# A convolution in rows from shifted copies, in the state-space stage of a hybrid decoder layer

## The chip, the cores and the metric

The kernel runs on one core of a Trainium2 chip. The metric is the device time of one execution in microseconds; of three runs the median counts.

## What is computed

One decoder layer for 256 tokens of width 2048, in float32. x is normalised, projected by one wide matrix, and goes through two mixers, a Mamba-2 branch and a differential attention; both are merged and projected, and a SwiGLU network follows. The change lies in the Mamba-2 branch:

```
xbc = silu(causal_depthwise_conv(xbc, conv_w, conv_b))      # 4 taps along the sequence
xs, Bm, Cm = split(xbc, ...)                                 # xs: 8 groups x 8 heads x 64
dt = softplus(dt_raw + dt_bias);  A = -exp(a_log)
y = ssd_chunked(xs, dt, A, Bm, Cm) + d_skip * xs             # one chunk of 256 tokens
# in it: cb = C @ B^T;  y_diag = (cb * decay) @ (xs * dt),  decay = exp(a_cs[l] - a_cs[s]) for l >= s
y = y * silu(z);  y = y * rsqrt(mean(y * y over the group) + eps) * norm_w
```

The convolution makes out[t, c] = b[c] + sum over j of w[j, c] * x[t - 3 + j, c], with nothing before t = 0.

## The kernel before

Every large product is made in **units**: two blocks of 128 rows of the weights by 512 columns. SP loads a unit's weights (512 KB) into one of four ring slots, w_raw (`load`, line 410). ScalarE rounds them to w_hi (`split_hi`, L724), VectorE makes the remainder w_lo (`split_lo`, L1257), and TensorE multiplies twelve times (`rows_unit`, L2246): high by high, high by low, low by high, for two blocks of the rows and two tiles of 128 tokens. A slot of w_hi is written once the unit four back has been multiplied (mm_done), a slot of w_raw once its remainder is made (lo_ready). So ScalarE and VectorE run up to four units ahead of TensorE. Each engine carries out its instructions in order, and semaphores are all that ties them together: the code of every engine says after which unit u of which chunk each small step stands.

The stage that is changed loops over eight groups g. A group is 16 units: eight make the x columns of the group (chunk x, into acc 0) and eight the z columns (chunk z, into acc 1). I call them x0 to x7 and z0 to z7. Because of the lead of four, the step that ScalarE or VectorE has "at u" of a chunk stands behind the split of the unit four later: u = 0 of chunk z behind the split of z4, u = 4 of chunk z behind that of the next group's x0. On TensorE "at u" is behind unit u itself. On SP the last load of chunk z stands at u = 7.

What happens to a group beside its units:

- ScalarE evicts chunk x, scaled by each token's factor, to x_proj, in rows (tokens on partitions). TensorE turns it into columns (channels on partitions) by eight transposes into acc 0, after z0. ScalarE writes the last tap and the bias from there to conv_x (`conv_first_taps`), VectorE adds the other three taps (`conv_taps`, L1447, twelve operations, one input in PSUM), the shift along the sequence being a shift along the free dimension. ScalarE applies silu, and after z4 TensorE turns conv_x back into rows by eight transposes. VectorE multiplies them by dt (xdt, L1682), ScalarE copies them to y_row, and GpSimd multiplies that by d_skip (L2199).
- GpSimd loads a_cs by broadcast from DRAM (acs_b, L2185) and adds a mask (L2193), ScalarE makes the decays by an exponential (`exps`, L977, at u = 2 and 3 of chunk z), VectorE multiplies them by cb (`decays`, L1658, at u = 3 and 4).
- In chunk x of the next group TensorE makes the decay products (`y_products`, L2549) after x1, ScalarE copies them out, and after x3 TensorE makes `y_rows` (transposes, and the product L2562). VectorE adds and gates (`tail_gated`), ScalarE sums the squares, GpSimd makes the factor, VectorE applies it (`tail_normed`, L1624), TensorE turns it into columns after z0, VectorE stores them to yT.

A VectorE operation that reads what the one before it wrote waits for that by a semaphore (`link`).

Of the kernel before, what the change touches and what calls it, by code (L numbers as in the profile page):

```python
# [28 lines left out]
ALU = mybir.AluOpType  # L29
# [3 lines left out]
P = 128  # L33
T = 256
# [150 lines left out]
def layer(nc, x, mix_norm_w, w_in, conv_w, conv_b, dt_bias, a_log, d_skip, ssm_norm_w, w_ssm_proj,  # L185
# [3 lines left out]
    with ctx:  # L189
# [6 lines left out]
        def sem(name):  # L196
# [77 lines left out]
        conv_x = at("conv_x", 191, [P, CT, T])  # L274
# [66 lines left out]
        conv_first, conv_done = sem("conv_first"), sem("conv_done")  # L341
        sq_read = sem("sq_read")
        bc_rows_ready, bc_T, x_rows_ready, x_T = sem("bc_rows_ready"), sem("bc_T"), sem("x_rows_ready"), sem("x_T")
# [14 lines left out]
        xs_ready, xs_T, xdt_ready, xrow_ready, skip_ready = (sem(n) for n in (  # L358
            "xs_ready", "xs_T", "xdt_ready", "xrow_ready", "skip_ready"))
# [39 lines left out]
        def _(sp):  # L399
# [302 lines left out]
        def _(act):  # L702
# [232 lines left out]

            def tail_columns(g):
# [4 lines left out]
            def x_chunk(g, head):  # L941
                for u in range(UPC):
                    split_hi()
                    if u == 1 and not head:
                        tail_columns(g - 1)
# [8 lines left out]
                    if u == 4 and not head:  # L954
                        tail_squares(g - 1)
# [10 lines left out]
                last.then_inc(x_rows_ready, 1)  # L966

            def exps(g, hf, head):

                act.wait_ge(acs_masked, g * 2 + (hf + 1))  # L970
                if hf == 0 and not head:
# [9 lines left out]
            def z_chunk(g, head):  # L981
                for u in range(UPC):
                    split_hi()
                    if u == 0:

                        act.wait_ge(x_T, g + 1)
                        for n in range(CT):
                            last = conv_first_taps(sums(0)[:, n], g * CT, conv_x[:, n], n)
                        last.then_inc(conv_first, 1)
# [3 lines left out]
                    if u == 2:  # L993
                        act.wait_ge(conv_done, g + 1)
                        nc.scalar.activation(conv_x[:], conv_x[:], ACT.Silu).then_inc(xs_ready, 1)
                        exps(g, 0, head)
                    if u == 3:
                        exps(g, 1, head)
                    if u == 5:

                        act.wait_ge(xdt_ready, g + 1)
                        nc.scalar.activation(y_row[:], side[:, 2:4], ACT.Copy).then_inc(xrow_ready, 1)
# [14 lines left out]
            for c in range(4):  # L1017
                for u in range(UPC):
                    split_hi()
                    if c == 0 and u == 1:  # L1020
# [1793 lines left out]
```

## Time and profile before

| what | value |
|---|---|
| median of three runs | 2049.43 us (2049.01 to 2050.93) |
| profiled execution | 2051.72 us, span of the trace 2050.1 us |
| busy share TensorE, VectorE, ScalarE, GpSimd | 100%, 76%, 57%, 8% |
| granted TensorE clock | 1.00 |
| DMA | 419.80 MB, 205 GB/s on average |
| the changed stage | about 592 to 1024 us of the span |

The span is the time from the first to the last instruction of the profiled execution. TensorE is busy nearly all the time, so the other engines' busy shares say little by themselves: what counts is whether each step is there when TensorE comes to it.

### The profile page before, as it was taken

Reading aid. Unit: us, or ns where it says so; the run is one execution under the profiler, and the core shown is the slowest. Engines: PE = TensorE matmul, PEld = TensorE weight load, DVE = VectorE, ACT = ScalarE, POOL = GpSimd, SP = SyncE. Lnnn points to the kernel's source line nnn. Section 1 sums busy time; section 2 is a strip of 40 time slices with the busy share of each in tenths; the row PEclk is TensorE's granted clock in tenths of the full one; section 3 lists DMA queues with packets and bytes.
Section 4 is the critical chain, followed back from the end, with each engine's and each line's share of the span. In section 5 each row is a group of like instructions: output and inputs, shape, how many; then the busy total and the mean of one; then the engine's idle time right before and its main releaser. Section 6 shows DMA issues by size and latency. Waiting matters only on the chain.

```text
span 2050.1 us, 28075 instructions
## 1 busy us (share of the span) xinstructions
PE 2040.8 (100%) x9580; PEld 1677.7 (82%) x9580; DVE 1566.3 (76%) x1861; ACT 1172.0 (57%) x1496; POOL 171.6 (8%) x195
## 2 busy tenths in 40 slices
PE   9999999999999999999999999999999999999999
PEld 8888877778888888888888888888888888887887
DVE  6777866665856777777667887888898889877866
ACT  5444655555556666666655554556666666645543
POOL 1121000000011222222000000010000000000000
PEclk9999999999999999999999999999999999999999
DMA  7656675654566666666565657598888888667574
GB/s 250 199 182 203 188 220 166 176 162 152 182 204 186 185 185 184 185 190 187 167 192 183 212 168 238 177 307 244 258 254 237 250 259 250 196 205 232 176 246 154
DMA packets 220626, 419.80 MB, mean 205 GB/s; under 512 B 16449, under 2 KB 22002, under 8 KB 220290
## 3 DMA queue, kind: packets, MB, share of 16 engines
q1 hardware_dynamic: 212162, 399.48, 61.8%
q0 software_dynamic: 7776, 18.94, 4.4%
q8 instruction: 47, 0.77, 0.2%
q10 hardware_dynamic: 608, 0.34, 0.1%
q14 instruction: 33, 0.27, 0.0%
HBM read 410.25 MB, written 4.26 MB: 202 GB/s over the span
## 4 chain that ended last, share of the span: by engine, by line
PE 92%; DVE 3%; DMA 2%; ACT 1%; issue 0%; SPq 0%; DVEq 0%; ACTq 0%
PE acc L2246 72%; PE side L2333 8%; PE acc L2333 6%; PE side L2262 3%; DMA w_raw<-in_w_ffn_down 1%; DVE w_lo L2038 1%; PE side L2402 1%; PE side L2549 1%; DVE w_raw L1953 0%; ACT w_hi L1216 0%; DVE w_lo L1257 0%; DMA x_row<-in_x 0%; DMA w_raw<-in_w_in 0%; PE acc L2262 0%; ACT w_hi L724 0%
## 5 line engine op out<-in xcount | busy, mean ns | idle before, releaser
L1257 DVE TENSOR_TENSOR w_lo<-w_raw,w_hi 128x1024 fp32r<-128x1024 f32 x332 | 420.7, 1280 | 245.7 <-ACT w_hi L724 244.5
L724 ACT ACTIVATE w_hi<-w_raw 128x1024 fp32r<-128x1024 f32 x332 | 348.5, 1057 | 355.7 <-PE acc L2246 315.2
L2246 PE MATMUL acc<-w_hi,h_hi 128*128 128x512 f32 x1248 | 498.7, 400 | 0.2
L2246 PE MATMUL acc<-w_hi,h_lo 128*128 128x512 f32 x1248 | 487.0, 390 | 0.0
L2246 PE MATMUL acc<-w_lo,h_hi 128*128 128x512 f32 x1248 | 485.9, 389 | 0.0
L2246 PEld LDWEIGHTS acc<-w_hi,h_hi 128*128 128x128 f32 x1248 | 234.4, 188 | 52.7 <-issue 7.0
L2246 PEld LDWEIGHTS acc<-w_hi,h_lo 128*128 128x128 f32 x1248 | 234.3, 188 | 50.3
L2246 PEld LDWEIGHTS acc<-w_lo,h_hi 128*128 128x128 f32 x1248 | 234.7, 188 | 47.6 <-issue 1.9
L1932 DVE TENSOR_TENSOR w_lo<-w_raw,w_hi 128x1024 fp32r<-128x1024 f32 x136 | 165.1, 1220 | 38.0 <-ACT w_hi L1137 35.4
L1053 ACT ACTIVATE w_hi<-w_raw 128x1024 fp32r<-128x1024 f32 x110 | 116.6, 1061 | 117.2 <-PE acc L2246 70.2
L1137 ACT ACTIVATE w_hi<-w_raw 128x1024 fp32r<-128x1024 f32 x136 | 142.9, 1057 | 65.8 <-PE acc L2246 50.4
L1216 ACT ACTIVATE w_hi<-w_raw 128x1024 fp32r<-128x1024 f32 x102 | 107.8, 1060 | 106.5 <-DMA w_raw<-in_w_ffn_down 57.4
L1734 DVE TENSOR_TENSOR w_lo<-w_raw,w_hi 128x1024 fp32r<-128x1024 f32 x110 | 132.2, 1223 | 47.3 <-ACT w_hi L1053 45.4
L1137 ACT ACTIVATE w_hi<-side_raw 128x1024 fp32r<-128x1024 f32 x100 | 106.2, 1062 | 98.1 <-PE acc L2246 45.2
L2038 DVE TENSOR_TENSOR w_lo<-w_raw,w_hi 128x1024 fp32r<-128x1024 f32 x102 | 122.6, 1223 | 47.9 <-ACT w_hi L1216 46.8
L2246 PE MATMUL acc<-w_hi,x2T_hi 128*128 128x512 f32 x384 | 150.9, 393 | 0.5 <-DVE w_lo L1932 0.5
L2246 PE MATMUL acc<-w_hi,x2T_lo 128*128 128x512 f32 x384 | 149.6, 389 | 0.0
L2246 PE MATMUL acc<-w_lo,x2T_hi 128*128 128x512 f32 x384 | 149.4, 389 | 0.0
L1932 DVE TENSOR_TENSOR w_lo<-side_raw,w_hi 128x1024 fp32r<-128x1024 f32 x100 | 122.1, 1221 | 18.3 <-ACT w_hi L1137 16.6
L2246 PE MATMUL acc<-w_hi,a_hi 128*128 128x512 f32 x252 | 98.2, 390 | 0.0
L2246 PE MATMUL acc<-w_hi,a_lo 128*128 128x512 f32 x252 | 98.1, 389 | 0.0
L2246 PE MATMUL acc<-w_lo,a_hi 128*128 128x512 f32 x252 | 98.1, 389 | 0.0
(436 smaller groups left out, 3445.9 us busy)
## 6 DMA issues: line engine op xcount, KB each, us to landing
w_raw<-in_w_in SPq DMA_DIRECT2D x320, 512.0 KB, 4.3
w_raw<-in_w_ffn_down SPq DMA_DIRECT2D x88, 512.0 KB, 4.9
w_raw<-in_w_ffn_gate SPq DMA_DIRECT2D x68, 512.0 KB, 4.6
w_raw<-in_w_ffn_up SPq DMA_DIRECT2D x68, 512.0 KB, 5.2
w_raw<-in_w_ssm_proj SPq DMA_DIRECT2D x64, 512.0 KB, 4.4
side_raw<-in_w_ffn_up SPq DMA_DIRECT2D x40, 512.0 KB, 4.7
w_raw<-in_w_attn_proj SPq DMA_DIRECT2D x32, 512.0 KB, 3.7
w_raw<-in_w_out SPq DMA_DIRECT2D x32, 512.0 KB, 4.7
```

The source lines that it names most:

```text
L724: nc.scalar.activation(w_hi[:, r], w_raw[:, n % RING], ACT.Copy).then_inc(hi_ready, 1)
L1053: nc.scalar.activation(w_hi[:, unit.slot % RING], w_raw[:, source], ACT.Copy).then_inc(hi_ready, 1)
L1137: nc.scalar.activation(w_hi[:, unit.slot % RING], ffn_source(names, name), ACT.Copy).then_inc(hi_ready, 1)
L1216: nc.scalar.activation(w_hi[:, unit.slot % RING], w_raw[:, source], ACT.Copy).then_inc(hi_ready, 1)
L1257: nc.vector.tensor_tensor(w_lo[:, r], w_raw[:, n % RING], w_hi[:, r].bitcast(F32), ALU.subtract).then_inc(lo_ready, 1)
L1734: nc.vector.tensor_tensor(w_lo[:, r], w_raw[:, source], w_hi[:, r].bitcast(F32), ALU.subtract).then_inc(lo_ready, 1)
L1932: nc.vector.tensor_tensor(w_lo[:, r], ffn_source(names, names[n]), w_hi[:, r].bitcast(F32), ALU.subtract).then_inc(lo_ready, 1)
L2038: nc.vector.tensor_tensor(w_lo[:, r], w_raw[:, source], w_hi[:, r].bitcast(F32), ALU.subtract).then_inc(lo_ready, 1)
L2246: done = nc.tensor.matmul(acc[p][:, t], a[:, k0 + kk, cut], w[:, r, kk], start=first and kk == n == 0, stop=last and kk == UK - 1 and n == ...
L2262: return nc.tensor.transpose(out_at, in_, ident)
L2333: done = nc.tensor.matmul(out_at, a, w[:, r, kk], start=first and kk == n == 0, stop=last and kk == UK - 1 and n == 2, skip_group_check=se ...
L2402: last = nc.tensor.matmul(side[:, 1 + m, first:first + width], qkT[half, 0, q * P:(q + 1) * P], qkT[half, 1, 0:width], start=True, stop=True)
```

## The change

The convolution is made in rows. With tokens on partitions, the row one, two or three tokens earlier lies on another partition, so SP copies x_proj from SBUF to SBUF, shifted by one, two and three partitions, into three tiles `earlier`. Partitions 16 to 127 of each go in three copies of 448 KB, then comes the weight load of z7, then six small copies: rows up to partition 15, and the first rows of the second tile of tokens from the last partitions of the first. VectorE sets the rows before t = 0 to zero once. GpSimd loads the group's taps and bias by broadcast over the partitions (`taps_load`, 4 x 2 KB and 2 KB a partition). VectorE multiplies each of the four tiles by its taps and adds them and the bias: eight operations over 128 x 1024 with both inputs in SBUF, behind the splits at u = 2 to 5 of chunk z. ScalarE applies silu in place at u = 6. So the sixteen transposes per group, conv_x, the taps' evictions and the copy to y_row are gone; xdt and the skip product read x_proj.

Moved: the exponentials from u = 2 and 3 to 4 and 5 (they also wait for taps_read, since taps_b lies in decay's place), the decay products with cb on VectorE from 3 and 4 to 6 and 7, xdt from u = 5 of chunk z to u = 0 of the next chunk x, y_products from x1 to x4, y_rows from x3 to x6, the gated tail from 3 to 6, the squares from u = 4 of chunk x to u = 0 of chunk z, y's scaling from VectorE (u = 6 of chunk x) to ScalarE (u = 2 of chunk z), y's transposes from z0 to z3, their store from u = 1 to 4. acc 0 is freed by ScalarE after the eviction. On GpSimd the order becomes: loads, skip, masks, wait for y_sum, taps, tail.

```diff
 SP, group i
-                chunk(w_in, (i + i) * (CW // 2) + COL_Z)
+                for u in range(UPC):
+                    if u == UPC - 1:
+                        sp.wait_ge(x_rows_ready, i + 1)
+                        for back in range(1, TAPS):
+                            sp.dma_start(earlier[back - 1][16:P], x_proj[16 - back:P - back]).then_inc(shift_in, 16)
+                    load(w_in, u * UK, (i + i) * (CW // 2) + COL_Z)
+                for back in range(1, TAPS):
+                    sp.dma_start(earlier[back - 1][back:16], x_proj[0:16 - back]).then_inc(shift_in, 16)
+                    sp.dma_start(earlier[back - 1][0:back, 1], x_proj[P - back:P, 0]).then_inc(shift_in, 16)
...
 ScalarE
+            def conv_silu(g):
+                act.wait_ge(conv_ready, g + 1)
+                nc.scalar.activation(x_proj[:], x_proj[:], ACT.Silu).then_inc(xs_ready, 1)
+            def tail_normed(g):
+                act.wait_ge(y_rstd, g + 1)
+                for t in range(TT):
+                    last = nc.scalar.activation(y_row[:, t], y_row[:, t], ACT.Copy, scale=y_scale[:, t:t + 1])
+                last.then_inc(y_ready, 1)
...
+                if not head:
+                    act.wait_ge(xdt_ready, g)
+                    act.wait_ge(skip_ready, g)
                 for t in range(TT):
                     last = nc.scalar.activation(x_proj[:, t], acc[0][:, t], ACT.Copy, scale=x_rstd[:, t:t + 1])
...
             def exps(g, hf, head):
                 act.wait_ge(acs_masked, g * 2 + (hf + 1))
+                if hf == 0:
+                    act.wait_ge(taps_read, g + 1)
...
+                    if u == 0 and not head:
+                        tail_squares(g - 1)
+                    if u == 2 and not head:
+                        tail_normed(g - 1)
+                    if u in (4, 5):
+                        exps(g, u - 4, head)
+                    if u == 6:
+                        conv_silu(g)
...
 VectorE
+            def by_taps(tile, back):
+                return nc.vector.tensor_tensor(tile[:], tile[:], taps_b[:, TAPS - 1 - back].unsqueeze(1).broadcast_to([P, TT, CW]), ALU.mult)
+            def conv_step(g, u):
+                if u == 2:
+                    dve.wait_ge(shift_in, g * 144 + 144)
+                    dve.wait_ge(taps_in, g * 32 + 32)
+                    by_taps(earlier[0], 1)
+                    by_taps(earlier[1], 2)
+                if u == 3:
+                    by_taps(earlier[2], 3)
+                    by_taps(x_proj, 0).then_inc(taps_read, 1)
+                if u == 4:
+                    dve.wait_ge(taps_read, g + 1)
+                    nc.vector.tensor_tensor(earlier[0][:], earlier[0][:], earlier[1][:], ALU.add)
+                    link(nc.vector.tensor_tensor(x_proj[:], x_proj[:], earlier[2][:], ALU.add))
+                if u == 5:
+                    link(nc.vector.tensor_tensor(x_proj[:], x_proj[:], earlier[0][:], ALU.add))
+                    nc.vector.tensor_tensor(x_proj[:], x_proj[:], conv_bias_b[:].broadcast_to([P, TT, CW]), ALU.add).then_inc(conv_ready, 1)
+            def tail_step(g, u):
+                if u == 0:
+                    x_scaled(g)
+                if u == 6:
+                    tail_gated(g)
...
+                    if u == 4 and not head:
                         tail_transposed(g - 1)
+                    conv_step(g, u)
+                    if u in (6, 7):
+                        decays(g, u - 6)
...
 GpSimd
+            def taps_load(g):
+                ours = conv_w[0][:, bass.ds(g * CW, CW)]
+                pool.dma_start(taps_b[:], ours.partition_broadcast(P)).then_inc(taps_in, 16)
+                pool.dma_start(conv_bias_b[:], conv_b[:, bass.ds(g * CW, CW)].partition_broadcast(P)).then_inc(taps_in, 16)
...
+            def next_group(i, first=False):
                 pool.wait_ge(decay_exp, i * 2 + 2)
                 loads(i + 1)
+                skip(i, first)
+                masks(i + 1)
+                pool.wait_ge(y_sum, i + 1)
+                taps_load(i + 1)
                 tail(i)
...
 TensorE
-                    if u == 1:
+                    if u == 4:
                         y_products(g)
-                    if u == 3:
+                    if u == 6:
                         y_rows(g)
...
-                        if not first:
-                            y_columns(g - 1)
-                    if u == 4:
-                        pe.wait_ge(xs_ready, g + 1)
-                        if not first:
-                            pe.wait_ge(yT_ready, g)
-                        for n in range(CT):
-                            for t in range(TT):
-                                last = transpose(side[:, 2 + t, n * P:(n + 1) * P], conv_x[:, n, t * P:(t + 1) * P])
-                        last.then_inc(xs_T, 1)
+                    if u == 3 and not first:
+                        y_columns(g - 1)
+                    if u == 6 and not first:
+                        pe.wait_ge(yT_ready, g)
```

## Rows read from the trace of the kernel before

**Rows 1.** Windows: us, busy us by engine, PEclk, DMA share, GB/s.

```profile
697.50:702.00 4.50, 4.50 (x21) 3.70 (x21) 2.87 (x3) 2.86 (x3) 0.00 (x0) 1.00 0.95 289
702.00:705.00 3.00, 3.00 (x17) 2.27 (x16) 1.20 (x2) 1.06 (x1) 0.00 (x0) 1.00 1.03 387
755.54:806.30 50.76, 50.76 (x264) 42.04 (x263) 37.58 (x40) 32.63 (x51) 11.70 (x9) 1.00 0.61 188
```

**Rows 2.** Chain of waits, one group: start us, length us, what.

```profile
704.79 13.65 PE acc L2246 x60
718.44 0.87 PE acc L2262 x8
...
720.84 10.91 PE acc L2246 x48
731.75 0.87 PE side L2262 x8
...
746.24 1.90 PE side L2549 x32
...
753.81 0.88 PE side L2262 x8
754.68 0.86 PE side L2562 x2
```

**Rows 3.** ScalarE's timeline, same group: start us, us, operation.

```profile
715.75 1.06 ACT L724 ACTIVATE w_hi<-w_raw 128x1024 fp32r<-128x1024 f32 x1 [1.35 <-PE acc L2246]
716.72 1.25 ACT L965 ACTIVATE x_proj<-acc,small 128x512 f32<-128x512 f32 x2
...
727.31 1.04 ACT L995 ACTIVATE conv_x<-conv_x 128x1024 f32<-128x1024 f32 x1
728.37 1.28 ACT L977 ACT_TABLE_LOAD   x1
729.67 2.45 ACT L977 ACTIVATE decay<-acs_b,neg_acs 128x128 f32<-128x128 f32 x8
```

**Rows 4.** VectorE's timeline, same group.

```profile
706.23 1.22 DVE L1614 TENSOR_TENSOR y_row<-side,y_row 128x1024 f32<-128x1024 f32 x1
707.48 0.69 DVE L1616 TENSOR_TENSOR y_row<-xdt_end,y_row 128x512 f32<-128x512 f32 x1
...
711.79 1.22 DVE L1257 TENSOR_TENSOR w_lo<-w_raw,w_hi 128x1024 fp32r<-128x1024 f32 x1 [1.22 <-ACT w_hi L724]
714.13 2.23 DVE L1257 TENSOR_TENSOR w_lo<-w_raw,w_hi 128x1024 fp32r<-128x1024 f32 x1 [1.11 <-ACT w_hi L724]
716.28 3.02 DVE L1624 TENSOR_SCALAR y_row<-y_row,small 128x512 f32<-128x512 f32 x2
...
721.66 5.24 DVE L1447 SCALAR_TENSOR_TENSOR conv_x<-acc,taps,conv_x 128x255 f32<-128x255 f32 x12
...
738.67 1.22 DVE L1257 TENSOR_TENSOR w_lo<-w_raw,w_hi 128x1024 fp32r<-128x1024 f32 x1
739.81 1.28 DVE L1682 TENSOR_TENSOR xdt<-side,dt 128x512 f32<-128x512 f32 x2
...
743.13 3.31 DVE L1257 TENSOR_TENSOR w_lo<-w_raw,w_hi 128x1024 fp32r<-128x1024 f32 x2 [1.22 <-ACT w_hi L724]
```

**Rows 5.** GpSimd's timeline, same group.

```profile
712.13 6.49 POOL L2193 TENSOR_TENSOR acs_b<-acs_b,cst 128x1024 f32<-128x1024 f32 x2
742.33 3.03 POOL L2199 TENSOR_TENSOR y_row<-y_row,d_skip_b 128x512 f32<-128x512 f32 x2 [23.71 <-ACT y_row L1002]
745.30 1.16 POOL L2185 DMA_DIRECT2D acs_b<-acs_scratch  x2
```

**Rows 6.** DMA issues: queue, count, size, median us to landing.

```profile
w_raw<-in_w_in SPq DMA_DIRECT2D x320, 512.0 KB, 4.3
...
acs_b<-acs_scratch POOLq DMA_DIRECT2D x16, 512.0 KB, 6.8
```

**Rows 7.** Line 410: ns min, median, max of an issue.

```profile
L410 SPq DMA_DIRECT2D w_raw<-in_w_in x320: 367/373/2333, 1.4 to 1067.5; - x160
```

More of the change, by code:

```diff
@@ L273, in layer @@
         x_proj = at("x_proj", 187, [P, TT, CW])
-        conv_x = at("conv_x", 191, [P, CT, T])
+        earlier = [at(f"earlier{n + 1}", kb, [P, TT, CW]) for n, kb in enumerate((138, 142, 175))]
+        taps_b = at("taps_b", 167, [P, TAPS, CW])
+        conv_bias_b = at("conv_bias_b", 191, [P, 1, CW])
         y_row = at("y_row", 195, [P, TT, CW])
@@ L1602, in _ @@
                 nc.vector.tensor_tensor(gated, acc[c % 2][:], gated, ALU.mult).then_inc(acc_free[c % 2], 1)
+            for back in range(1, TAPS):
+                last = nc.vector.memset(earlier[back - 1][0:back, 0], 0.0)
+            link(last)
             def tail_gated(g):
@@ new lines, in x_scaled @@
+            def x_scaled(g):
+                by_head = "p (h d) -> p h d"
+                dve.wait_ge(xs_ready, g + 1)
+                for t in range(TT):
+                    last = nc.vector.tensor_tensor(
+                        xdt[:, t].rearrange(by_head, d=HP), x_proj[:, t].rearrange(by_head, d=HP),
+                        dt[:, t, bass.ds(g * HG, HG)].unsqueeze(2).broadcast_to([P, HG, HP]), ALU.mult)
+                last.then_inc(xdt_ready, 1)
+                dve.wait_ge(xdt_ready, g + 1)
+                nc.vector.tensor_tensor(
+                    xdt_end[:].rearrange(by_head, d=HP), xdt[:, 0].rearrange(by_head, d=HP),
+                    edge[:, 0, bass.ds(g * HG, HG)].unsqueeze(2).broadcast_to([P, HG, HP]), ALU.mult).then_inc(xdt_end_ready, 1)
@@ L1694, in _, with z_chunk @@
+            def z_chunk(g, head):
+                for u in range(UPC):
+                    split_lo()
+                    if u == 4 and not head:
+                        tail_transposed(g - 1)
+                    conv_step(g, u)
+                    if u in (6, 7):
+                        decays(g, u - 6)
             x_chunk(0, True)
+            dve.wait_ge(edge_ready, 1)
             z_chunk(0, True)
@@ L2205, in _ @@
             pool.dma_start(acs_dram[:], acsT[:]).then_inc(acs_out, 16)
+            taps_load(0)
             pool.wait_ge(acs_out, 16)
             loads(0)
[L2208 to L2209 removed]
+            masks(0)
+            def next_group(i, first=False):
                 pool.wait_ge(decay_exp, i * 2 + 2)
                 loads(i + 1)
+                skip(i, first)
+                masks(i + 1)
+                pool.wait_ge(y_sum, i + 1)
+                taps_load(i + 1)
                 tail(i)
[L2214 removed]
+            next_group(0, True)
+            with repeat(pool, G - 2, [(own, 2)]) as i:
+                next_group(i + 1)
+            skip(G - 1)
             tail(G - 1)
```

118 lines of the change are left out of this document (26 added, 92 removed).

## The prediction

> **What bounds the kernel now.** First the windows view of one group of the stage that the change touches: TensorE is busy 50.76 of 50.76 us at full granted clock, VectorE 37.6, ScalarE 32.6, GpSimd 11.7, the DMA engines 61% [rows 1]. Then the chain of waits over one group: only TensorE, with nothing between its pieces [rows 2]. A group's period is therefore TensorE's work: 16 units, 13.65 us for five, so 2.72 each and 43.5 in all, and 7.2 us of small products and transposes between them. Last, the timelines of ScalarE, VectorE and GpSimd [rows 3 to 5], to see how far ahead of TensorE they run. That decides this change: it takes work from TensorE and gives VectorE more.
>
> The lead: ScalarE starts a unit's high part 0.2 us after the matmuls of the unit four back are done, and takes 1.06; VectorE's low part takes another 1.14 (the step from one operation to the next; the listed 1.22 overlap) [rows 3, 4]. TensorE needs it 3 units = 8.16 us after that same boundary, so VectorE may be 5.7 us late before TensorE stops.
>
> **TensorE's part.** Out go eight transposes of x_proj and eight of conv_x per group, 0.87 us each lot [rows 2]. The number of breaks in the matmul stream stays four (after units z0, z3, x4, x6), so what a break costs remains. Gain 1.74 us a group, 8 groups: 13.9 us. Period 50.76 - 1.74 = 49.0 if nobody stops TensorE.
>
> **The clock of one group.** I set T=0 where unit x7 ends and z0 begins, and put the new order on it. TensorE: z0 done 2.7; the scores and the break cost 0.66 + 0.1 (718.44 to 720.84 in the old group, less two lots of 0.87 [rows 2]); z1 done 6.2, z2 8.9, z3 11.6; y's transposes 1.0; z4 15.3, z5 18.1, z6 20.8, z7 23.5, x0 26.2, x1 28.9, x2 31.7, x3 34.4, x4 37.1. There the decay products stand, 1.97 with their break; after x6, y's rows, 1.8.
>
> **Copies.** ScalarE evicts x_proj at 1.2 to 2.4 as before (1.25 us [rows 3]). SP waits for that in front of the last z load, which it could otherwise issue at 2.8 (low part of z3), so the load is only 1 us later and isn't needed before 11.8: free. The copies carry 3 x 112 x 4 KB and small ones, 1.56 MB, a resource of which before has no like; the load adds 0.52. At 387 GB/s (a burst of weight loads) that is 5.4 us; GpSimd's new taps load (1.31 MB of broadcast) goes out at y's sum, -2.7. Its like is acs_b: 1.05 MB that land 6.8 us after issue [rows 6], in the burst that moves 289 GB/s [rows 1]; 3.6 us of that is data, so 3.2 are lead, and the taps' data start at 0.5, just ahead of the copies, and take 4.5. 0.5 + 4.5 + 5.4 + 0.5 of completion (my estimate) = 10.9; all of it at 289 gives 12.7; no clash gives 9.5. VectorE asks for the copies after its low part of z6, at 11.35. I take 0.3 us of waiting, nearer to the first value since most of the bytes are no broadcast, bounds 0 and 1.4; a copy from SBUF to SBUF at half the rate would make it 3.5. SP issues a load in 0.37 us [rows 7], so nine copies hold it some 4 us; the next load, x0, wanted landed by 15.5, goes out at 6.5 and lands at 10.8 by the median of 4.3 [rows 6], some 3 us later behind the queue: free.
>
> **VectorE.** Its tail of group g-1 comes at x6: y's sum is there at -2.7, low z2 ends at -2.1, four operations take 3.7, so low z3 ends at 2.8 and it then idles in wait of TensorE. Out: twelve tap steps (5.24) and y's scaling (3.02, of which 0.95 is work) [rows 4]; the latter goes to ScalarE at z2, ready at 11.3, and TensorE asks at 11.6: free by a hair. In: four products and four sums of 128x1024, 1.14 each, 1.25 where a wait for its own result follows (706.23 to 707.48) [rows 4]. In order from 11.35: product, product, low z7, product, product (17.05: taps_read), low x0, y's columns, sum, sum (21.7), low x1 (its high part comes at 21.9, since the exponentials now wait for taps_read, then take 1.28 + 2.36 [rows 3]), sum, sum (25.5), low x2, decay product (27.7). ScalarE's silu needs a table load and 1.04, ready 27.9, high part of x3 at 28.85.
>
> **Who shares with GpSimd.** GpSimd is given skip (two halves) once x is ready at 27.9, and masks when acs_b has landed: loads issued 24.3, 6.8 us [rows 6], 31.1. In the trace such an operation and one of VectorE with two SBUF inputs exclude each other and take turns [rows 4, 5]: a low part ends at 713.01, the next one, started at 714.13, ends at 716.36 having worked its own 1.1, so the first mask ran from 713.0 to 715.3; the second has 716.36 to 718.62, and the scaling started at 716.28 gets nowhere until then. So 2.27 us of VectorE's time for a mask. For a skip half 1.0: the pair lasts 3.03 with one low part in between, and two low parts beside it take 3.31 instead of 2.36. The old tap steps read PSUM and one SBUF tile; twelve went by in 5.24 us, none stretched. All the new ones read two SBUF tiles, and x's scaling by dt now does too. So after 27.7: skip half (to 29.0), low x3 30.15, skip half, decay product 32.3, mask, low x4 35.7, mask, x's scaling 1.28: done at 39.3. If the masks come later they still fall before it.
>
> The Trainium skill has this as a rule ("SBUF — State Buffer", Who interferes with whom): a VectorE instruction with two SBUF inputs contends with a GpSimd one that reads SBUF, whoever issues second blocks fully, and one with a single SBUF input doesn't contend. The rows agree, and it speaks against this change, which turns one-input work into two-input work. Without that rule the chain would end 5.5 us earlier, and the first rival would be the forecast.
>
> **Sum.** TensorE reaches the decay products at 37.1 and gets xdt at 39.3: 2.2 us lost a group, part of it already at x4 (35.7 against 34.4). Against that stands 1.74. The stall falls on groups 1 to 6: 13.2. Group 0 has no y columns on VectorE: 1.1. Group 7 has no masks behind it: none. Waiting for copies 7 x 0.3 = 2.1. Together -13.9 + 14.3 + 2.1 = +2.5 us. The profiled execution's span of 2050.1 becomes 2052.6 and its time of 2051.72 becomes 2054.2; that time stands 2.3 above the median of 2049.43, so the median becomes 2051.9, say 2052. Free, by what hides them: masks are done at 38 and used 28 us later; GpSimd has issued taps by -1.3 and the sums of squares that its tail waits for come at 5.2; TensorE's new wait for yT at z6 (19.4 against 20.8); the eviction's new wait for xdt and skip (both done ten us before it); ScalarE's wait for conv_ready, behind which high x3 is queued (28.9, low part 30.15, wanted 31.7; if GpSimd takes one turn more there, 1 us appears at x3 and is the same us that is lost later). ScalarE's lost evictions (y_row, first taps) pay for nothing, as it isn't late where they stood; its table loads stay two a group.
>
> **Rivals.**
> 1. VectorE comes in time and all of the gain shows. For: it was idle 13 of 50.8 us, and needs only 37.6 - 5.2 - 3.0 + 9.3 = 38.7 of 49. Against: its idle time lies at 3 to 10, before the copies are there; behind them it must run 17 operations plus GpSimd's turns in 25.7 us. It would take GpSimd's masks to land behind x's scaling (9 us instead of 6.8 from issue) or an alternation kinder than the one read. 2049.4 - 13.9 = 2035.5; half of it, 2043.
> 2. Slower: the copies land late. Every us beyond 11.35 moves the whole VectorE chain and costs 7 us in all; from 0.6 us it is slower by over 0.2%. Place: the wait after low z6. With copies at half the rate, landed at 13.5 to 14.8: 2052 + 13 to 22, 2065 to 2074 at the end. For: broadcast and copies meet on the same DMA engines, and the small ones come last. Against: a burst reaches 387 GB/s. The Trainium skill ("DMA: Bandwidth & Descriptors", Anatomy of one DMA) gives each DMA some 2 us of fixed cost; nine in a row would be 18 us and a far larger stall. Loads that land in 4.3 us while one goes out every 2.7 overlap theirs, so I leave that out.
> 3. A weight load or y's scaling is late by the new traffic (margins 3 us and 0.3 us): TensorE then stops at z3 too, but part is given back at x4. 2054 to 2060.
> That the change doesn't do what it says is no rival: the transposes are gone from the instruction stream.
>
> **How the numbers follow.** Measurement tells 0.2%, 4 us. Forecast (chain ends 2.2 late) 45%, own range 2046 to 2057; rival 1 25%; rival 2 22%; rival 3 8%. The range takes rival 1 down to 2037 and rival 2 up to 2065. Faster by over 0.2% (under 2045.3): rival 1 and a sliver, 28%. Slower (over 2053.5): rivals 2 and 3 and the upper end of the forecast, 36%. Within: 36%.
>
> **What would show it.** Right: the sixteen transposes gone; TensorE idle about 2 us a group, ahead of the decay products, released by VectorE's xdt or w_lo; period 51 us; VectorE without a gap from the shift wait to x's scaling; its operations beside masks stretched by 2 us. Rival 1: period 49.0, no wait. Rival 2: VectorE's first tap product waits for DMA for over 0.6 us. Wrong at the root: new two-input products that take another time than 1.14, or masks that land elsewhere.

## The result: 3.4% slower, and the profile after

The changed kernel takes 2119.65 us (median; 2114.64 to 2122.49), the kernel before 2050.11 on the same chip: ratio 1.0337, 95% interval 1.0316 to 1.0358. That is 69.5 us slower, and outside the range. The profiled execution has a span of 2120.9 us and a mean granted clock of 0.986.

The windows view of one group of the changed stage, where [rows 1] had 50.76 us. The first row is the whole group, the others are pieces of it. Columns as there: us, busy us of TensorE, its weight loads, VectorE, ScalarE, GpSimd, granted clock, DMA share, GB/s.

```profile
787.04:847.48 60.44, 53.00 (x247) 42.31 (x247) 42.67 (x35) 31.50 (x49) 13.31 (x11) 0.94 0.74 204
...
803.40:806.00 2.60, 2.53 (x13) 2.25 (x14) 0.05 (x1) 0.02 (x1) 0.00 (x0) 0.78 1.05 228
806.00:810.00 4.00, 4.00 (x14) 3.16 (x14) 0.00 (x0) 0.08 (x1) 0.00 (x0) 0.71 1.05 224
...
814.30:818.90 4.60, 0.12 (x2) 0.07 (x1) 4.60 (x5) 2.29 (x5) 0.00 (x0) 0.96 0.44 119
818.90:824.00 5.10, 5.10 (x16) 4.10 (x17) 4.72 (x5) 5.10 (x15) 0.00 (x0) 0.70 0.39 104
```

A group takes 60.44 us instead of the forecast 51.2. TensorE is idle for 7.44 of them, and busy for 53.00 instead of 49.0, most of it because its granted clock is down behind its two stops. The DMA engines are busy all the time from 803.4 to 810 and move only 224 to 228 GB/s; the burst of [rows 1] moved 387 at nearly the same share.

The waits of the whole run, by who waited for what: us in total, times, longest.

```profile
PE acc L2292 <- DVE yT L1652: 45.9, 7, 7.8
PE side L2308 <- ACT y_row L956: 6.9, 5, 2.1
PE acc L2292 <- DVE w_lo L1281: 5.3, 7, 2.2
...
DVE earlier L1666 <- DMA earlier<-x_proj: 61.3, 8, 9.1
...
ACT w_hi L735 <- DMA w_raw<-in_w_in: 146.4, 58, 7.9
```

Before, the last of these was 33.6 us in 18 times. The wait that costs is the one for yT, at z6: the prediction had listed it as free.

The timelines of the same group show why. T, the end of x7, is 789.75. SP first, then VectorE, then ScalarE (start us, length us, operation, in brackets the idle time before it and what ended it):

```profile
792.08 3.15 SPq L496 DMA_DIRECT2D earlier<-x_proj  x3
795.49 0.62 SPq L412 DMA_DIRECT2D w_raw<-in_w_in  x1
796.16 0.89 SPq L499 DMA_DIRECT2D earlier<-x_proj  x1
...
800.18 0.69 SPq L500 DMA_DIRECT2D earlier<-x_proj  x1
```

```profile
802.23 1.23 DVE L1281 TENSOR_TENSOR w_lo<-w_raw,w_hi 128x1024 fp32r<-128x1024 f32 x1 [3.95 <-ACT w_hi L735]
810.67 2.36 DVE L1666 TENSOR_TENSOR earlier<-earlier,taps_b 128x1024 f32<-128x1024 f32 x2 [7.21 <-DMA earlier<-x_proj]
...
817.49 1.22 DVE L1652 TENSOR_TENSOR yT<-side,cols 128x1024 f32 x1
```

```profile
801.14 1.06 ACT L735 ACTIVATE w_hi<-w_raw 128x1024 fp32r<-128x1024 f32 x1 [3.74 <-DMA w_raw<-in_w_in]
802.10 1.32 ACT L956 ACTIVATE y_row<-y_row,small 128x512 f32<-128x512 f32 x2
809.92 1.06 ACT L735 ACTIVATE w_hi<-w_raw 128x1024 fp32r<-128x1024 f32 x1 [6.50 <-DMA w_raw<-in_w_in]
```

The large copies go out at T + 2.3, as forecast. SP is done with the last small one at T + 11.1 and the first product starts at T + 20.9; forecast: copies there at 10.9. In the groups around this one it is T + 19.8 and T + 20.4. The weight load between the copies, issued at T + 5.7, is read by ScalarE only at T + 20.2, and the load before it is late as well (3.74 us), behind which y's scaling stood: so TensorE stops a first time, for y_row. Then it stops for yT, which VectorE makes only after six operations that stand behind the copies (four products and two low parts).

The DMA issues of that stage (queue, count, size, median us from issue to landing; the nine copies on SP have none listed), to be read against [rows 6]:

```profile
w_raw<-in_w_in SPq DMA_DIRECT2D x320, 512.0 KB, 4.5
...
taps_b<-in_conv_w POOLq DMA_DIRECT2D x8, 1024.0 KB, 10.6
acs_b<-acs_scratch POOLq DMA_DIRECT2D x16, 512.0 KB, 6.0
conv_bias_b<-in_conv_b POOLq DMA_DIRECT2D x8, 256.0 KB, 12.9
```

The taps, issued at 787.70, are the new thing here: 1 MB that takes 10.6 us, so they move until 798.3 (the bias, by its median, until 801.4). The large copies are issued from 792.08 on, and VectorE gets them at 810.67: the broadcast lies over the first third of that time (with the bias, the first half) and over two weight loads, and it is over when the engines move 224 to 228 GB/s.

### The profile page after: what moved, and what is told of

It is laid out like the page before. It is cut to its first block, busy times and chain, and to the rows that moved or that the text cites. A ratio compares the mean times of both kernels' runs of the same rounds, so it can differ in the third digit from the quotient of the medians.

```text
span 2120.9 us, 27734 instructions
## 1 busy us (share of the span) xinstructions
PE 2052.2 (97%) x9452; PEld 1675.7 (79%) x9452; DVE 1601.4 (76%) x1816; ACT 1158.0 (55%) x1470; POOL 182.4 (9%) x211
## 4 chain that ended last, share of the span: by engine, by line
PE 66%; issue 9%; DVE 9%; DMA 6%; ACT 4%; SPq 3%; POOL 1%; DVEq 0%; ACTq 0%; POOLq 0%
PE acc L2292 50%; PE side L2379 7%; PE acc L2379 5%; DMA earlier<-x_proj 3%; PE side L2308 2%; DMA w_raw<-in_w_ffn_down 1%; SPq L496 1%; DVE w_lo L2064 1%; DVE w_lo L1281 1%; SPq L499 1%; POOL small L2173 1%; DMA w_raw<-in_w_in 1%; DVE earlier L1666 1%; ACT w_hi L735 1%; ACT decay L1007 1%
## 5 line engine op out<-in xcount | busy, mean ns | idle before, releaser
L2292 PE MATMUL acc<-w_hi,h_hi 128*128 128x512 f32 x1248 | 508.6, 408 | 51.7 <-DVE yT L1652 45.9
L2292 PE MATMUL acc<-w_hi,h_lo 128*128 128x512 f32 x1248 | 493.5, 395 | 0.0
L2292 PE MATMUL acc<-w_lo,h_hi 128*128 128x512 f32 x1248 | 493.1, 395 | 0.0
L2292 PEld LDWEIGHTS acc<-w_hi,h_hi 128*128 128x128 f32 x1248 | 238.9, 191 | 113.0 <-issue 54.9
L2292 PEld LDWEIGHTS acc<-w_lo,h_hi 128*128 128x128 f32 x1248 | 239.4, 192 | 48.6 <-issue 1.9
L1958 DVE TENSOR_TENSOR w_lo<-w_raw,w_hi 128x1024 fp32r<-128x1024 f32 x136 | 165.2, 1222 | 38.1 <-ACT w_hi L1161 35.4
```

Source lines behind the costliest of these rows:

```text
L1958: nc.vector.tensor_tensor(w_lo[:, r], ffn_source(names, names[n]), w_hi[:, r].bitcast(F32), ALU.subtract).then_inc(lo_ready, 1)
L2292: done = nc.tensor.matmul(acc[p][:, t], a[:, k0 + kk, cut], w[:, r, kk], start=first and kk == n == 0, stop=last and kk == UK - 1 and n == ...
```

## Experiments

All are given as medians with the ratio to the kernel before, which ran beside them at 2050.7 to 2051.9 us. They come in the order of the argument. "The kernel after" is the changed one.

### Is the rest of the timetable right? The copies out, then the masks too

The nine copies and the waits for them are out (the tiles are cleared once), the rest stays.

```diff
-                        for back in range(1, TAPS):
-                            sp.dma_start(earlier[back - 1][16:P], x_proj[16 - back:P - back]).then_inc(shift_in, 16)
...
-                    dve.wait_ge(shift_in, g * 144 + 144)
```

> The changed kernel without the nine copies and without SP's and VectorE's waits for them (the tiles are cleared once, so the earlier taps see zeros; all else as changed). Theory 1, the copies' landing is the loss and the rest goes by the forecast's timetable: TensorE reaches the decay products 2.2 us too early in six groups, 1.1 in one, so 2050 +- 3; with y's scaling late by the taps' broadcast as in the changed kernel's trace (2 us a group) up to 2060. Theory 2, GpSimd's turns cost nothing: 2036. Theory 3, the copies are only part, the new order of waits (yT at z6, broadcast) loses by itself: 2080 or more.

Measured: 2051.33 us, ratio 0.9998 (0.9988 to 1.0007). The stage's period is 51.2 us on average over six groups (evictions of chunk x start at 665.77 and 973.16; one period is 50.7 to 51.7), forecast 51.2. VectorE and GpSimd in one group, T = 767.94:

```profile
799.28 6.71 POOL L2217 TENSOR_TENSOR acs_b<-acs_b,cst 128x1024 f32<-128x1024 f32 x2
...
798.33 2.06 DVE L1655 TENSOR_TENSOR decay<-decay,cb 128x1024 f32<-128x1024 f32 x1
800.32 3.42 DVE L1273 TENSOR_TENSOR w_lo<-w_raw,w_hi 128x1024 fp32r<-128x1024 f32 x1
803.66 3.48 DVE L1682 TENSOR_TENSOR xdt<-x_proj,dt 128x512 f32<-128x512 f32 x2
```

A low part takes 3.42 us instead of 1.22, x's scaling 3.48 instead of 1.28, and xdt is done at T + 39.2, forecast 39.3. The broadcast of the taps still runs in this kernel and lands 10.1 us after issue: ScalarE waits for weights more than before (93.9 us in 51 times, before 33.6), but TensorE hardly: 1.9 us in all for y_row. So the broadcast alone, without copies beside it, costs next to nothing.

Then, besides, GpSimd's addition of the mask is replaced by the mere signal (and the exponential takes no bias):

```diff
-                    nc.gpsimd.tensor_tensor(blocks, blocks, mask, ALU.add).then_inc(acs_masked, 1)
+                    nc.gpsimd.sem_inc(acs_masked, 1)
```

> As e1_no_copies, and GpSimd's masks are left out too (and the exponentials' bias with them, so the decays are other numbers). Theory 1 (masks hold VectorE off for 2 x 2.27 us ahead of xdt, which is the chain's 2.2 us): the stall before the decay products is gone, 13 to 15 us faster than e1, about 2036. Theory 2 (turns cost nothing): as e1 within 3 us.

Measured: 2034.44 us, 0.9924 (0.9907 to 0.9940). From the second group on the evictions of chunk x stand 49.03 us apart, in every group the same; forecast period without a stall 49.0, time 2035.5. The masks thus cost 2.2 us a period, as forecast. By the medians they cost 16.9 us, a little over the 13 to 15 expected; group 0 alone loses 2.3 us (48.47 against 46.13), where the prediction had 1.1. So the gain of the change, the loss by taking turns with GpSimd and the order of VectorE's chain were priced right in the main; what is missing comes with the copies.

### What makes the copies late: shift, amount, or what lies beside them

Same copies, same bytes, but each partition copied onto itself, the small copies likewise (no token is shifted, so the convolution is another).

```diff
-sp.dma_start(earlier[back - 1][16:P], x_proj[16 - back:P - back])
+sp.dma_start(earlier[back - 1][16:P], x_proj[16:P])
```

> The changed kernel with all nine copies of the same sizes and destinations, but from the same partitions (no shift, so the convolution is another). Theory A, moving from one partition to another makes the 4 KB rows slow (15 bytes per ns and engine against 24 of a weight load): landing 2 to 3 us earlier, 2095 to 2105. Theory B, a copy from SBUF to SBUF has that rate in any case: 2119 +- 4.

Measured: 2121.01 us, 1.0330 (1.0309 to 1.0351), 1.4 us from the kernel after, with ranges that overlap. Theory B: going to another partition costs nothing that can be seen.

The taps and the bias are loaded once, for group 0, and every product uses the bias row, so nothing is broadcast in the groups.

```diff
-                taps_load(i + 1)
...
-                    dve.wait_ge(taps_in, g * 32 + 32)
+                    dve.wait_ge(taps_in, 32)
```

> The changed kernel with the taps and bias loaded once and not per group (all products use the first group's bias row, so the convolution is another). Theory A, the broadcast takes the DMA engines from 790 to 800 us of the trace, just before the copies: they land 5 us earlier a group and y's scaling is no longer late, 5 to 7 us a group, about 2070. Theory B, the copies' own rate and SP's issues decide: z load and copies land at most 1 us earlier, 2105 to 2119.

Measured: 2076.69 us, 1.0128 (1.0111 to 1.0145): 43.0 of the 69.5 us are gone (expected: 2070, or 2105 and more). The waits that are left:

```profile
PE acc L2291 <- DVE w_lo L1281: 17.5, 12, 2.3
PE acc L2291 <- DVE yT L1652: 5.9, 7, 1.2
...
DVE earlier L1666 <- DMA earlier<-x_proj: 21.5, 8, 6.7
```

The wait for yT falls from 45.9 to 5.9 us, and VectorE's for the copies from 61.3 to 21.5. Of these, 6.7 us fall in group 0: its copies come at T + 17 in this kernel too, though its taps, issued at 593.9, are in long before. In the other groups the first product now starts at T + 13.1 to 13.7 (in the one read here 791.91, with T = 778.64, so 13.3): without any broadcast in their way the copies are still 2 us later than VectorE asks. The windows view of the time in which they move:

```profile
781.90:787.20 5.30, 5.30 (x26) 4.38 (x25) 2.45 (x2) 3.27 (x7) 1.11 (x3) 1.00 0.95 252
```

The same kernel, each copy a quarter as wide (128 of 512 columns; the rest of the tiles stays zero), as many copies and instructions:

```diff
-sp.dma_start(earlier[back - 1][16:P], x_proj[16 - back:P - back])
+sp.dma_start(earlier[back - 1][16:P, :, 0:CW // 4], x_proj[16 - back:P - back, :, 0:CW // 4])
```

> e3_taps_once with nine copies of a quarter of the columns (the rest of the taps sees zeros). Same number of issues, a quarter of the bytes. Theory A (issuing decides): within 5 us of e3, 2072 to 2080. Theory B (data decide): VectorE's wait vanishes, 2050 to 2056.

Measured: 2049.69 us, 0.9991 (0.9982 to 1.0001), 27.0 us less, and VectorE waits for copies once, 0.8 us. Theory B; this is the time of the kernel with no copies at all (2051.3). SP still issues all nine, over 7.6 us (769.56 to 777.17). So what is left of the lateness is data, not the number of copies or SP's time for them.

And the other way round: the kernel before with the nine copies added, into tiles that nobody reads.

```diff
+                    if u == UPC - 1:
+                        sp.wait_ge(x_rows_ready, i + 1)
+                        for back in range(1, TAPS):
+                            sp.dma_start(earlier[back - 1][16:P], x_proj[16 - back:P - back]).then_inc(shift_in, 16)
                     load(w_in, u * UK, (i + i) * (CW // 2) + COL_Z)
```

> The kernel before, with the nine copies of every group added as SP issues them in the changed one and nobody waiting for them. Theory A, the loss comes through VectorE's wait for the copies alone: at most 4 us slower than before. Theory B, the copies' traffic and SP's 8.7 us of issuing delay weight loads z7, x0 and x1 beyond their slack: 15 us slower or more.

Measured: 2050.93 us, 1.0000 (0.9990 to 1.0010). Theory A. The traffic by itself and SP's issuing slow nothing that TensorE waits for; ScalarE's waits for weights are even (31.6 us, before 33.6). The copies cost only through whoever waits for them, and through the broadcast beside them.

### The broadcast: its place or its form

The broadcast goes out earlier, after GpSimd's masks, well before T instead of 2 us before it (y_cols is put elsewhere in SBUF for that).

```diff
-                pool.wait_ge(y_sum, i + 1)
+                pool.wait_ge(y_cols_sum, i + (LAMBDAS + 1))
                 taps_load(i + 1)
```

> The changed kernel, with the taps' broadcast issued once the decay products are done (some 7 us earlier) instead of after y's sum; y_cols moves to x_proj's place so that the taps' place is free by then. Theory A, the broadcast costs by meeting z6's load and the copies: as e3_taps_once, 2077 +- 5. Theory B, its bytes cost wherever they are: 2095 or more.

Measured: 2104.33 us, 1.0261 (1.0244 to 1.0278), 15.3 us less than the kernel after instead of 43: Theory B. VectorE's wait for copies is that of the kernel without broadcasts (21.3 us), but now the weight loads before T are late. ScalarE:

```profile
775.20 1.06 ACT L735 ACTIVATE w_hi<-w_raw 128x1024 fp32r<-128x1024 f32 x1 [3.02 <-DMA w_raw<-in_w_in]
780.60 1.06 ACT L735 ACTIVATE w_hi<-w_raw 128x1024 fp32r<-128x1024 f32 x1 [2.77 <-DMA w_raw<-in_w_in]
789.28 1.06 ACT L735 ACTIVATE w_hi<-w_raw 128x1024 fp32r<-128x1024 f32 x1 [7.62 <-DMA w_raw<-in_w_in]
```

The taps were issued at 777.42. The weights of the last of these three waited 7.62 us, and TensorE waited 22.7 us in six groups for what stands behind them on ScalarE and VectorE (y_row). The broadcast does harm in this place too.

To that, the six small copies go out by GpSimd, beside SP's large ones.

```diff
-                    sp.dma_start(earlier[back - 1][back:16], x_proj[0:16 - back]).then_inc(shift_in, 16)
+                    pool.dma_start(earlier[back - 1][back:16], x_proj[0:16 - back]).then_inc(small_in, 16)
```

> e5 with the six small copies issued by GpSimd, beside SP's large ones. In e3 VectorE still waited 2.7 us a group for the copies. Theory A, that is SP's issuing (nine copies in 8.7 us, the last issued at T+10.5): the wait is gone or under 0.5 us, 2051 to 2056, as e1_no_copies. Theory B, it is the large copies' data (1.38 MB at 240 GB/s, behind them z7's load): 2068 to 2077.

Measured: 2100.42 us, 1.0239 (1.0222 to 1.0256). VectorE's wait for copies is nearly gone (4.7 us, once), the time isn't: TensorE's waits for y_row rise to 31.5 us in seven groups. Both theories missed it, 2051 to 2056 and 2068 to 2077, since both left out the weight loads that the moved broadcast delays. It only shows that the copies were no longer what ended last.

The same kernel, but the taps' load reads 128 different rows of w_in, as many bytes, and so does the bias's (the convolution uses these numbers instead):

```diff
-pool.dma_start(taps_b[:], ours.partition_broadcast(P))
+pool.dma_start(taps_b[:], w_in[0, 0:P, bass.ds(g * CW, TAPS * CW)].rearrange("p (j c) -> p j c", j=TAPS))
```

> e6_small_on_gpsimd with the taps' load replaced by one of the same size from 128 different rows of w_in (other values, so the convolution is another). In e6 the broadcast takes 10 us and the weight load issued beside it 11, with 275 GB/s moved meanwhile. Theory A, reading the same rows for every partition is slow: the load lands in under 6 us, TensorE waits less for y_added, 2060 to 2075. Theory B, any 1.3 MB beside the weight loads costs that: 2095 to 2105.

Measured: 2064.99 us, 1.0062 (1.0045 to 1.0079), 35.4 us less, in Theory A's range, though the load lands in 6.7 us and not in under 6. The rows are now 8 KB and different. To tell these two apart, a broadcast again, of one row of 8 KB: the taps of a group are gathered once at the start into a DRAM scratch. The layer is computed in full.

```diff
+pool.dma_start(packed.rearrange("g (j c) -> g j c", c=CW), conv_w[0][:, 0:DI].rearrange("j (g c) -> g j c", c=CW))
...
-ours = conv_w[0][:, bass.ds(g * CW, CW)]
+ours = packed[bass.ds(g, 1), :]
```

> e6_small_on_gpsimd with the taps gathered once in DRAM so that a group's four rows are one piece of 8 KB per partition, as acs_b's are 4 KB pieces. acs_b's 1.05 MB lands in 6 us, the taps' 1.05 MB in 10. Theory A, the 2 KB rows of a broadcast are its slow part: lands in 6 to 7 us, 2065 to 2080. Theory B, the size of the pieces does nothing: 2100 +- 4.

Measured: 2070.74 us, 1.0090 (1.0073 to 1.0107), 29.7 us less than with rows of 2 KB: Theory A. The landing, in the three kernels in this order (2 KB rows, 128 different rows, one row of 8 KB):

```profile
taps_b<-in_conv_w POOLq DMA_DIRECT2D x8, 1024.0 KB, 10.2
```

```profile
taps_b<-in_w_in POOLq DMA_DIRECT2D x8, 1024.0 KB, 6.7
```

```profile
taps_b<-packed_taps POOLq DMA_DIRECT2D x8, 1024.0 KB, 6.8
```

That 128 partitions read the same row is cheap (5.7 us, with the bias's in it, which is still a broadcast here); that it comes as four rows of 2 KB costs most. (The four rows also lie far apart in DRAM, and the packed row in another tensor; neither is separated from the length of the rows.) Whether that holds too where the change puts the load was tried last, with the packed taps as the only edit to the kernel after:

> The kernel after with one change: the taps are gathered once into a DRAM scratch, 8 KB in a row for each group, and each group's load broadcasts that one row (128 rows of 8 KB instead of 512 of 2 KB). Place in the order, copies and bytes are as in the kernel after (2119.7). Theory A, the 2 KB rows of the broadcast are its slow part wherever it stands: the taps land some 7 us after issue instead of 10.6, and the time falls by the 30 us that the same step gave behind the earlier place (2100.4 to 2070.7): 2086 to 2094. Theory B, behind y's sum the broadcast meets the copies with any row size, since the bytes are the same: it falls by less than 12 us, 2108 or more. VectorE's wait for the copies is 9.1 us a group in the kernel after; A wants 4 to 5.

Measured: 2092.72 us, 1.0205 (1.0190 to 1.0221), 26.9 us less; landing 6.5 us; VectorE waits for copies 41.6 us instead of 61.3; from the second group on the first product starts at T + 15.6 to 19.5. Theory A, with 5.2 us of that wait a group where it wanted 4 to 5. The same three microseconds, T + 0.25 to T + 3.25, when the taps move, in the kernel after and in this one:

```profile
790.00:793.00 3.00, 3.00 (x17) 2.52 (x15) 2.91 (x3) 2.50 (x4) 0.00 (x0) 1.00 0.89 170
```

```profile
782.00:785.00 3.00, 3.00 (x17) 2.52 (x15) 2.69 (x3) 2.49 (x4) 0.00 (x0) 1.00 0.93 347
```

With rows of 2 KB the DMA engines are as busy and move half: 170 GB/s against 347. This is one group; over the seven groups from the second on the same three microseconds have 136 to 265 GB/s against 294 to 367. What is not moved then is moved later, beside the copies. Here too the wait for yT carries what is left:

```profile
PE acc L2296 <- DVE yT L1654: 30.1, 7, 5.0
PE acc L2296 <- DVE w_lo L1283: 5.4, 5, 2.3
PE side L2312 <- ACT y_row L958: 4.2, 3, 2.0
```

### Is there a version that beats the kernel before?

Taps loaded once, as above, and the small copies on GpSimd:

> e3_taps_once with the six small copies issued by GpSimd. Theory A, with neither the broadcast nor the queue of small copies behind z7's load the copies are there when VectorE asks: as e1_no_copies, 2050 to 2055. Theory B, the large copies' data alone are late: 2065 or more.

Measured: 2067.60 us, 1.0082 (1.0065 to 1.0099). By its time theory B, but not by its reason. With the small copies on GpSimd's queue the landings are listed:

```profile
earlier<-x_proj SPq DMA_DIRECT2D x24, 448.0 KB, 6.1
earlier<-x_proj POOLq DMA_DIRECT2D x8, 6.0 KB, 7.1
```

The large copies are issued by T + 4.6, the small one of 6 KB, the last, at T + 5.6, and 7 us for 6 KB can't be its own data. In the group read here (T = 773.40) the last large copy, issued at 776.94, lands 8.1 us later, at T + 11.6; the last small one, issued at 779.03, lands 7.3 us later, at T + 13.0; and the first product starts then (786.39). So what VectorE waits for last is a small copy, and the large ones are late by a few tenths. From the second group on that is T + 11.9 to 14.1, instead of 13.1 to 13.7, and VectorE still waits 13.8 us in eight groups. Relieving SP of the small copies gives only 9.1 us. To this kernel, the end of the chain is moved later, so that TensorE asks for xdt 5 us later:

```diff
-                    if u == 4:
+                    if u == 6:
                         y_products(g)
-                    if u == 6:
+                    if u == 7:
                         y_rows(g)
...
-                    if u == 6:
+                    if u == 7:
                         conv_silu(g)
```

and the second decay product behind the split of x5, x's scaling behind x6, the gated tail behind x7.

> e12 with the chain's end moved later: second decay product behind the split of x5, xdt behind x6, silu behind x3's high part, decay products on TensorE after x6, y's rows and the gated tail after x7. The timetable has xdt done at 41.2 and TensorE asking at 42.5, and x6's low part 0.2 us late. Theory A, the timetable holds: the stall of e12 goes, 14 us faster than e12, 2036 to 2041. Theory B, the stall moves to the splits of x4 to x7: within 5 us of e12.

Measured: 2050.28 us, 0.9994 (0.9985 to 1.0004). It is 17.3 us faster for that, more than the 14 expected, but 9 us over 2041, the upper end of the time expected. A period is 50.05 us (716.85, 766.91, 816.96), one over the 49.03: the wait for w_lo is left (5.7 us in 11 times). The same with each group's own taps, packed:

> The kernel of the packed taps (taps early, small copies on GpSimd, 2070.7) with the end of the chain moved later as in the kernel that was 17 us faster by it: silu behind the split of x3, second decay product behind that of x5, x's scaling behind x6, the decay products behind unit x6 of TensorE, y's rows and the gated tail behind x7. ScalarE also waits for y's sum before it writes x_proj again. All of the layer is computed. Theory A, what is left of the loss in the packed kernel (20 us over before) is the same lateness of VectorE's chain as there: relief takes 14 to 18 us, 2053 to 2057, and no wait of TensorE's for xdt is left. Theory B, what is left are the weight loads that stand behind the broadcast (the waits for y_row and w_lo, 22 us in sum), which relief does not touch: 2064 or more. Faster than before would need the waits for w_lo to be gone too, 2045 or less; I give that 1 in 10.

Measured: 2055.80 us, 1.0022 (1.0013 to 1.0031), 14.9 us less than without the relief. Theory A. What is left:

```profile
PE acc L2310 <- DVE w_lo L1284: 10.4, 14, 1.8
PE acc L2310 <- DVE yT L1655: 3.7, 5, 1.0
```

So the convolution in rows, with the broadcast mended and the chain given more room, is 5 us over the kernel before; with no taps to load it is level. None of the versions that make all the copies beats it.

## Why the prediction was wrong, step by step

**TensorE's part: right.** 49.0 us a group were forecast; 49.03 were measured where nothing stopped it (copies and masks out), and the time was 2034.4 against 2035.5.

**VectorE's chain and GpSimd's turns: right.** Without the copies xdt was done at T + 39.2 (39.3), the masks ran to T + 38.05 (38), and the time was 2051.3, where the sum without its 2.1 us for the copies gives 2050. The forecast of 2052 was thus the time of a kernel whose copies are there in time. The Trainium skill ("SBUF — State Buffer", Who interferes with whom) calls the instruction that comes second fully blocked; the trace agrees, with one of VectorE's let in between two of GpSimd's (low part 3.42 us, then the scaling 3.48). On work with one input from SBUF the prediction read its rows wrong, which cost it nothing. The old tap steps are no evidence: they run from 721.66 to 726.9, and GpSimd's masks were over at 718.62 [rows 4, 5]. And y's scaling, which has one tile as its input and a factor for each partition, was held up by a mask for 2 us. So "the rows agree" holds for two inputs only; for one input the section makes an exception of VectorE's modes that use both ports, which the prediction leaves out.

**Copies: this step failed**, in three terms. They were to be there at T + 10.9, with 0.3 us of waiting a group. From the second group on VectorE gets them at T + 19.8 to 21.0, and it waits 6.6 to 9.1 us a group (5.7 in group 0).

1. *The taps' broadcast was mis-sized.* I took acs_b as its like, 1.05 MB at 289 GB/s, and let it be over at T + 5. But acs_b reads one run of 4 KB for each partition (four heads of 256 tokens), the taps four separate rows of 2 KB. It lands 10.6 us after issue. Its short rows cost 27 us (2119.7 to 2092.7) and the rest of it another 16 (to 2076.7, taps once).
2. *The rate of the copies was that of weight loads.* 387 GB/s was the best burst of [rows 1]. With no broadcast beside them the stretch with copies and loads moved 252 GB/s at a DMA share of 0.95, and the first product stood at T + 13.3, where the terms of my sum without the taps give T + 8.3 (issued at 2.4, 5.4 of data, 0.5 of completion; the 9.5 that the prediction has for no clash doesn't follow from them, and no run shows the 0.5). The range's upper bound, 12.7, was made with 289 GB/s for everything and is beaten too; half the rate, which stood in rival 2, was nearer. The Trainium skill ("DMA: Bandwidth & Descriptors", Where 436 GB/s comes from) puts the limit of transfers within SBUF at 435 GB/s; the windows shown, in which copies and loads move together, have 195 to 291, so the measurement decides. What limits them isn't shown: not the shift, and not SP's issuing.
3. *SP's issuing*: nine copies and the load hold it 8.8 us (792.08 to 800.87), not 4. The price [rows 7] was that of a weight load, 0.37; a small copy takes 0.65 to 0.89. This one matters little: the same nine, a quarter as wide, cost nothing.

**"The load is only 1 us later ... free"** and **"TensorE's new wait for yT at z6"**: both followed from that step. The load landed 14.4 us after its issue. And each free item was checked against copies that land in time; with copies at T + 20.9, yT, which VectorE makes behind them, is the first thing of that chain that TensorE misses, and it misses it by 4.5 us in the group shown and 7.8 in the worst.

**The rivals.** Rival 2 was the right mechanism in the right place, VectorE's first tap product waiting for DMA. Its price held roughly: "every us beyond 11.35 costs 7 us in all". From T + 13.3 (2076.7) to about T + 20.4 (2119.7) are 43 us for 7.1 us, 6 for each. From in time (2051.3) to T + 13.3 it is 25 for 2, which looks like more. The evictions of chunk x show where it falls: six periods grow from 51.2 to 53.6 us, 14 us in all, as the rule has it, and group 0, whose copies are more than 5 us late and not 2, from 48.5 to 56.2, another 8. Why group 0 is that late isn't shown. What was wrong was its end, T + 14.8 at the worst instead of 20.9. Its argument for ("broadcast and copies meet on the same DMA engines") outweighed the one against, a burst of another kind of transfer. What it cites from the Trainium skill, 2 us of fixed cost for each DMA, stands there in a section on DMAs issued by GpSimd, and these go out by SP; nine copies of a quarter's width were there in time, so a cost of 2 us for each in turn isn't seen. Rival 3 also happened, by its first sign (6.9 us for y_row).

**The clock was left out.** After each stop the granted clock falls to its lower level (1.2 GHz, 2.4 being full): after the 2.1 us for y_row it is down for 3.5 us, from 1.3 us behind the restart on; after the 4.5 us for yT it is down when TensorE goes on, and for 3.2 us from there. Then it is full again.

```profile
804.80:808.30 3.50, 3.50 (x11) 2.72 (x10) 0.00 (x0) 0.00 (x0) 0.00 (x0) 0.51 1.08 195
808.30:810.00 1.70, 1.70 (x9) 1.41 (x8) 0.00 (x0) 0.08 (x1) 0.00 (x0) 1.00 1.03 291
818.80:819.40 0.60, 0.56 (x1) 0.50 (x2) 0.60 (x1) 0.60 (x4) 0.00 (x0) 0.50 1.01 130
819.40:822.00 2.60, 2.60 (x8) 2.01 (x7) 2.26 (x3) 2.60 (x8) 0.00 (x0) 0.51 0.46 167
```

The busy time of the group is 4.0 us over the 49.0, and the clock's rows account for some 3.4 of it (half of 6.7 us). So about a third of what this group takes over 49.0 (11.4 us) isn't idle time but work done at the lower level; over six groups the busy time is 3.0 us a group too long and the idle time 7.9. In the copies' absence no group stopped for long and the clock stayed at 1.00, which is why the forecast got by without it.

The books, each a difference of two medians along one path from the kernel before to the kernel after: the gain -16.9 (before to copies and masks out), masks +16.9, copies' data +25.4 (no copies, with the broadcast, to taps once), the broadcast's long-row part +16.0, its short rows +26.9. The sum, +68.3, closes on the measured +69.5 by the way it is made, so it proves nothing; and copies and broadcast cost what they do only together. On another path the parts would be others.

## What to carry to other kernels

A transfer takes its price from a row with the same source, destination and length of contiguous pieces; where the trace has none, the upper bound is to be set wide (here 1.4 us of waiting were allowed, and 5.7 to 9.1 came), and everything that is queued behind the wait is priced with that bound. An operand that is broadcast in every round of a loop is worth gathering in DRAM into one contiguous row for each round (27 and 30 us here), and it is worth asking which weight loads it lies over: the one move tried here gave 15 us of 43 and made other loads late. A step that is "free by a hair" is to be checked against the late case of the step ahead of it.

## What the runs showed of the hardware

- 1 MB by broadcast to 128 partitions lands in 9.3 to 10.6 us (medians) from rows of 2 KB and in 6.5 to 7.4 us from one row of 8 KB; 128 different rows of 8 KB take 6.7. The short rows also slow what lies beside: one load of 512 KB was 14.4 us from issue to ScalarE's use of it, at a median of 4.5. In the same three microseconds of seven groups the DMA engines moved 136 to 265 GB/s with them and 294 to 367 with the long row, about equally busy.
- The DMA engines can be fully busy (share 1.05) at 224 GB/s with copies within SBUF and weight loads under way, the broadcast being over by then; weight loads alone had 387 at 1.03. A copy of 6 KB behind the large ones landed 7.1 us after issue.
- A copy that moves rows to other partitions costs as much as one that leaves them there (2121.0 and 2119.7 us).
- Behind stops of TensorE of 2.1 and 4.5 us the granted clock was 0.50 to 0.51 for 3.5 and 3.2 us. With shorter stops (taps once, none over 2.3 us) four of six groups still have a mean granted clock of 0.97, the other two 1.00.
- VectorE's work with two inputs in SBUF and GpSimd's take turns, one operation each (a low part 3.42 us instead of 1.22 beside a mask), and a scaling with one tile as input was held up the same way (3.02 us, of which 0.95 is work).
